# A ring of six weight places, with the low parts written over the weights

## The reference, cut to what matters

```
def reference(x, mem, ...):
    h = first_block(x, mem, ...)       # depth 1
    return second_block(h, ...)        # depth 2, then rmsnorm

first_block:   proj = rmsnorm(h) @ w_in                      # q, k, v, u
               h += concat(norm(attention(q, k, v)), norm(s5(u))) @ w_out
               h += memory_attention(rmsnorm(h), rmsnorm(mem))   # w_mem_q, _k, _v, _o
               h += peer(rmsnorm(h))
peer:          q = x @ w_peer_q;  scores against 2 x 128 keys, top 16 x 16 of 16384 experts
               sum_k gate[k] * gelu(x . u[k]) * v[k]
hybrid_layer:  proj = rmsnorm(x) @ w_in                      # 9 parts
               mixed = sum of 3:  sigmoid(gate) * (mixer(proj) @ w_mixer_out)   # ssd, mla, gdn
               h = x + mixed @ w_out
               return h + square(relu(rmsnorm(h) @ w_up)) @ w_down
```

## Time and profile before

| | |
|---|---|
| median of 3 runs | 5157.57 us (5157.56 to 5158.48) |
| profiled execution: its time, its span | 5149.14 us, 5147.2 us |
| mean granted TensorE clock, share of full speed | 0.983 |
| busy: PE, DVE, ACT, POOL | 4939.9, 2903.8, 1800.2, 704.3 us |
| DMA | 527.60 MB, mean 103 GB/s |

### The profile page before, as it was taken

The page is one execution under the profiler, slowest core; times in us unless marked ns, Lnnn a source line. Parts: engine busy times, 40 slices in busy tenths (PEclk is TensorE's granted clock), DMA queues, the critical chain, the costliest instruction groups (busy, mean ns, idle before and its releaser), DMA issues. The chain is left out here.

```text
span 5147.2 us, 62486 instructions
## 1 busy us (share of the span) xinstructions
PE 4939.9 (96%) x24184; PEld 4029.3 (78%) x24184; DVE 2903.8 (56%) x5300; ACT 1800.2 (35%) x2840; POOL 704.3 (14%) x494
## 2 busy tenths in 40 slices
PE   8979999999999999998999999999989999999999
PEld 6438688888887888877887777888878877777887
DVE  6676568888403544456546555553474466565533
ACT  3314433333322322233333334342333333343422
POOL 4641002233240000000300001000003100011000
PEclk9989999999999999998999999999999999999999
DMA  2012133555546555531022121322210221213222
GB/s 107 25 45 95 49 112 116 188 184 187 181 152 216 188 196 191 193 135 42 1 80 73 61 74 49 112 91 98 90 54 1 74 72 64 70 54 107 90 99 82
DMA packets 231733, 527.60 MB, mean 103 GB/s; under 512 B 19600, under 2 KB 89488, under 8 KB 230032
## 3 DMA queue, kind: packets, MB, share of 16 engines
q1 hardware_dynamic: 231440, 523.61, 29.9%
HBM read 448.03 MB, written 75.50 MB: 102 GB/s over the span
## 5 line engine op out<-in xcount | busy, mean ns | idle before, releaser
L552 DVE TENSOR_TENSOR weight_low<-ring,weight_high 128x1024 fp32r<-128x1024 f32 (+2 forms) x606 | 709.2, 1170 | 1230.0 <-PE banks L105 1164.8
L540 ACT CAST weight_high<-ring 128x1024 fp32r<-128x1024 f32 (+2 forms) x728 | 728.2, 1002 | 546.9 <-PE banks L105 518.9
L103 PE MATMUL banks<-x_high,weight_high 128*128 128x512 f32 x1856 | 758.7, 409 | 30.2 <-DVE weight_low L552 17.1
L552 POOL TENSOR_TENSOR weight_low<-ring,weight_high 128x1024 fp32r<-128x1024 f32 x122 | 301.0, 2468 | 3288.6 <-PE banks L105 2135.5
L105 PE MATMUL banks<-x_high,weight_low 128*128 128x512 f32 x1856 | 727.4, 392 | 0.0
L104 PE MATMUL banks<-x_low,weight_high 128*128 128x512 f32 x1856 | 727.0, 392 | 0.0
L103 PEld LDWEIGHTS banks<-x_high,weight_high 128*128 128x128 f32 x1856 | 351.3, 189 | 123.1 <-issue 26.8
L104 PEld LDWEIGHTS banks<-x_low,weight_high 128*128 128x128 f32 x1856 | 351.3, 189 | 82.0 <-issue 10.6
L103 PE MATMUL banks<-xn_high,weight_high 128*128 128x512 f32 x1024 | 410.5, 401 | 0.7 <-ACT hT L1744 0.7
L105 PEld LDWEIGHTS banks<-x_high,weight_low 128*128 128x128 f32 x1856 | 350.8, 189 | 74.6
L103 PE MATMUL banks<-act_high,weight_high 128*128 128x512 f32 x1024 | 399.0, 390 | 5.6 <-DVE act_low L1976 5.6
(11 more groups left out here) (638 smaller groups left out, 9099.1 us busy)
## 6 DMA issues: line engine op xcount, KB each, us to landing
ring<-in_peer_u SPq DMA_DIRECT2D x128, 512.0 KB, 3.3
ring<-in_peer_v SPq DMA_DIRECT2D x128, 512.0 KB, 3.4
acts<-dot_act SPq DMA_DIRECT2D x128, 256.0 KB, 2.0
gates<-gate_block SPq DMA_DIRECT2D x64, 512.0 KB, 4.6
ring<-in_w_up SPq DMA_DIRECT2D x64, 512.0 KB, 3.2
ring<-in_w_down SPq DMA_DIRECT2D x64, 512.0 KB, 3.2
activations<-acts SPq DMA_DIRECT2D x126, 256.0 KB, 3.7
gates_in<-gates SPq DMA_DIRECT2D x126, 256.0 KB, 3.9
```

Source lines behind the costliest of these rows:

```text
L103: nc.tensor.matmul(out, w_high, x_high, start=start, stop=False)
L540: self.nc.scalar.copy(self.wH[:, g % HIGHS, 0:kc * P], self.ring[:, g % SLOTS, 0:kc * P]).then_inc(self.high_made, 1)
L552: ops.tensor_tensor(self.wL[:, g % LOWS, 0:kc * P], self.ring[:, g % SLOTS, 0:kc * P], self.wH[:, g % HIGHS, 0:kc * P].bitcast(F32), ALU.s ...
```

## The change

The ring grows from four places to six, and the room for `weight_low` (two places) goes. The low part of tile g is written over the tile itself, in place g % 6. `ring_low` is a second name for the ring's memory, in the type that TensorE takes. So a load waits until TensorE has used tile g - 6, and a low part waits for nothing but its high part. In `linears` and `combine`, DVE makes both low parts of the stage that comes next, and POOL none. Whoever borrows the ring is given its first four places. There are now six semaphores for loads and six for low parts, where there were four and two.

```diff
-HIGHS, LOWS = 3, 2
+HIGHS, RING = 3, 6
@@ Weights
-        self.wL = held.enter_context(nc.sbuf_tensor("weight_low", [P, LOWS, D], F32R))
+        self.nc, self.ring, self.wL = nc, ring, ring_low
...
-        if g >= SLOTS:
-            self.wait_low(sp, g - SLOTS)
-        sp.dma_start(self.ring[:, g % SLOTS, 0:kc * P], row(w, at)).then_inc(self.loaded[g % SLOTS], 16)
+        if g >= RING:
+            sp.wait_ge(self.used, g - RING + 1)
+        sp.dma_start(self.ring[:, g % RING, 0:kc * P], row(w, at)).then_inc(self.loaded[g % RING], 16)
...
         eng.wait_ge(self.high_made, g + 1)
-        if g >= LOWS:
-            eng.wait_ge(self.used, g - LOWS + 1)
-        ops.tensor_tensor(self.wL[:, g % LOWS, 0:kc * P], self.ring[:, g % SLOTS, 0:kc * P],
-                          self.wH[:, g % HIGHS, 0:kc * P].bitcast(F32), ALU.subtract).then_inc(self.low_made[g % LOWS], 1)
+        ops.tensor_tensor(self.wL[:, g % RING, 0:kc * P], self.ring[:, g % RING, 0:kc * P],
+                          self.wH[:, g % HIGHS, 0:kc * P].bitcast(F32), ALU.subtract).then_inc(self.low_made[g % RING], 1)
@@ linears, gpsimd
-            if ahead:
-                weights.split_low(eng, nc.gpsimd, ahead.kc, base + total + 1)
@@ linears, vector
             for i in range(total):
-                if i + 2 <= total:
-                    lows(eng, nc.vector, i + 2)
-                elif ahead:
-                    weights.lows += 1
+                lows(eng, nc.vector, i + 2)
@@ combine
-            @block.gpsimd
-            def _(pool):
-                weights.split_low(pool, nc.gpsimd, ahead.kc, base + PK + 1)
...
                 weights.split_low(dve, v, ahead.kc)
-                weights.lows += 1
+                weights.split_low(dve, v, ahead.kc)
@@ program
-        ring = sb("ring", [P, SLOTS, 8 * P])
+        ring_at = nc.sbuf_base
+        ring = sb("ring", [P, RING, 8 * P])
+        ring_low = nc.alloc_sbuf_tensor_at("ring_low", [P, RING, 8 * P], F32R, offset=ring_at)
```

More of the change, by code:

```diff
@@ L508, with __init__ @@
 class Weights:
-    def __init__(self, nc, held, ring):
+    def __init__(self, nc, held, ring, ring_low):
         def sem(name):
             return held.enter_context(nc.semaphore(name))
-        self.nc, self.ring = nc, ring
+        self.nc, self.ring, self.wL = nc, ring, ring_low
         self.wH = held.enter_context(nc.sbuf_tensor("weight_high", [P, HIGHS, D], F32R))
-        self.wL = held.enter_context(nc.sbuf_tensor("weight_low", [P, LOWS, D], F32R))
-        self.loaded = [sem(f"weight{u}_loaded") for u in range(SLOTS)]
+        self.loaded = [sem(f"weight{u}_loaded") for u in range(RING)]
         self.high_made, self.used = sem("weight_high_made"), sem("weight_used")
-        self.low_made = [sem(f"weight_low{u}_made") for u in range(LOWS)]
+        self.low_made = [sem(f"weight_low{u}_made") for u in range(RING)]
         self.loads = self.highs = self.lows = self.placed = 0
@@ L530, in load @@
         g, self.loads = self.loads, self.loads + 1
-        if g >= SLOTS:
-            self.wait_low(sp, g - SLOTS)
-        sp.dma_start(self.ring[:, g % SLOTS, 0:kc * P], row(w, at)).then_inc(self.loaded[g % SLOTS], 16)
+        if g >= RING:
+            sp.wait_ge(self.used, g - RING + 1)
+        sp.dma_start(self.ring[:, g % RING, 0:kc * P], row(w, at)).then_inc(self.loaded[g % RING], 16)
     def split_high(self, act, kc):
         g, self.highs = self.highs, self.highs + 1
-        act.wait_ge(self.loaded[g % SLOTS], 16 * (g // SLOTS + 1))
+        act.wait_ge(self.loaded[g % RING], 16 * (g // RING + 1))
         if g >= HIGHS:
             act.wait_ge(self.used, g - HIGHS + 1)
-        self.nc.scalar.copy(self.wH[:, g % HIGHS, 0:kc * P], self.ring[:, g % SLOTS, 0:kc * P]).then_inc(self.high_made, 1)
+        self.nc.scalar.copy(self.wH[:, g % HIGHS, 0:kc * P], self.ring[:, g % RING, 0:kc * P]).then_inc(self.high_made, 1)
     def wait_low(self, eng, g):
-        eng.wait_ge(self.low_made[g % LOWS], g // LOWS + 1)
+        eng.wait_ge(self.low_made[g % RING], g // RING + 1)
     def split_low(self, eng, ops, kc, at=None):
@@ L549, in split_low @@
         eng.wait_ge(self.high_made, g + 1)
-        if g >= LOWS:
-            eng.wait_ge(self.used, g - LOWS + 1)
-        ops.tensor_tensor(self.wL[:, g % LOWS, 0:kc * P], self.ring[:, g % SLOTS, 0:kc * P],
-                          self.wH[:, g % HIGHS, 0:kc * P].bitcast(F32), ALU.subtract).then_inc(self.low_made[g % LOWS], 1)
+        ops.tensor_tensor(self.wL[:, g % RING, 0:kc * P], self.ring[:, g % RING, 0:kc * P],
+                          self.wH[:, g % HIGHS, 0:kc * P].bitcast(F32), ALU.subtract).then_inc(self.low_made[g % RING], 1)
     def parts(self, g, c):
         w = slice(c * P, (c + 1) * P)
-        return self.wH[:, g % HIGHS, w], self.wL[:, g % LOWS, w]
+        return self.wH[:, g % HIGHS, w], self.wL[:, g % RING, w]
     def clear(self):
@@ L948, in attention_memory @@
     return (scratch[:, 3:5, :], scratch[:, 5:8, :],
-            ring[:].rearrange("p s n -> p (s n)").rearrange("p (b k n) -> p b k n", b=2, k=4), spare[:, 0, 0:8])
+            ring[:, 0:SLOTS, :].rearrange("p s n -> p (s n)").rearrange("p (b k n) -> p b k n", b=2, k=4), spare[:, 0, 0:8])
 MIXED_FROM = 6
@@ L1457, in state_space @@
                                           tables.bim)
-    sets = [scratch[:], ring[:].rearrange("p s (two n) -> p (s two) n", two=2)]
+    sets = [scratch[:], ring[:, 0:SLOTS, :].rearrange("p s (two n) -> p (s two) n", two=2)]
     def by_half(x):
@@ L2646, in delta_rule @@
         kb = yT[:].rearrange("p c (t n) -> p c t n", n=P)[:, 4:8]
-        ring4 = ring[:].rearrange("p s (a t n) -> p s a t n", t=TT, n=P)
+        ring4 = ring[:, 0:SLOTS, :].rearrange("p s (a t n) -> p s a t n", t=TT, n=P)
         Dm = [ring4[:, 0, 0], ring4[:, 0, 1]]
@@ L2939, in program @@
         rstd = sb("rstd", [P, T])[:]
-        weights = Weights(nc, held, ring)
+        weights = Weights(nc, held, ring, ring_low)
         tools = (roots, eps, ident[:], columns, ones[:])
```

## The result

The kernel after takes 5191.28 us (median of 4 runs, 5190.06 to 5192.77) against 5157.57: ratio 1.0068, 95% interval 1.0056 to 1.0080. It is 0.7% slower; 5143.8 was forecast. The profiled execution took 5190.61 us, 41.5 more than that of before.

The account below looks back on a forecast made before the run. TensorE, busy 4939.9 of 5147.2 us, was taken as the bound. Stage ends 8.2 plus stalls inside stages 6.0 less clears 0.4 gave 13.8 us less: median 5143.8 from 5157.57, range 5138 to 5149, chance 0.70.

Parts of the forecast that it names:

- Writing in place.: DVE's low parts written over their source: from -0.02 to +0.02 us per low part, taken as 0.
- The rival on the slow side: DVE becomes last at the 16 stage-end barriers, late by a low part of 1.23 us: 5171.7 us, chance 0.04.
- all eight like rows 3: Eight stage ends like mem_in's, where POOL's low part comes last: idle 0.85 becomes 0.30, 4.4 us saved.
- mla_tail, two ends: Two stage ends where DVE comes last, slowed beside POOL: it ends 0.94 us sooner each, 1.9 saved.
- latents, two ends: Ends of the latents' stage: the new DVE low part delays the last eviction, yet restart comes sooner; 1.4 us saved.
- mem_in, first stall: Eviction in mem_in no longer stands behind a waiting low part; the 1.60 us stall shrinks by 1.1.
- gdn_tail, two layers: Low parts start without DVE's idle time of 0.47; the 2.82 us stall shrinks by 0.7, twice: 1.4 saved.
- ssd_tail, two layers: Stall of 2.10 us becomes 1.34, and the half-clock stretch behind it probably goes; 1.3 each, 2.6 saved.
- combine, 0.88: Low part in combine starts up to 3.01 us earlier, so TensorE's 0.88 wait for activations goes: 0.9 saved, once.
- six more clears: Six added semaphores are cleared at the program's end: cost 0 to 0.55 us, taken as 0.4.
- Stage ends: POOL's 16 low parts at stage ends go and DVE takes them over, shortening TensorE's idle time: 8.2 us saved together.
- gdn_in: Low part there starts with no idle time before it, so its stalls stay; nothing was counted.

Follow-up runs that it names:

- low_aligned: The kernel after with the table `columns` moved ahead of the ring, so low parts start at a multiple of 256 bytes: 5133.79 us, ratio 0.9959 to before.
- before_low_swapped: The kernel before with low parts placed ahead of the high parts, both at a multiple of 256 bytes: 5154.63 us, ratio 0.9997.
- aligned_pool_ends: The kernel after with aligned low parts, POOL again making the second low part at 16 stage ends, without waiting for TensorE: 5132.68 us, ratio 0.9958.
- pool_ends_late: The kernel after with aligned low parts, POOL making those 16 stage-end low parts and again waiting for TensorE's use two tiles before: 5143.62 us, ratio 0.9983.

## Why the prediction was wrong

**The step that failed: "Writing in place."** The prediction asked what the low part costs DVE, and got that right: "I take 0", and the mean of one 128x1024 low part on DVE is 1234 ns after and 1233 before. It never asked what the new place costs those who read from it. Each of the 5408 chunks of low parts that meet 512 columns is loaded by TensorE, the engine that bounds the kernel, and the sum took its matmuls as unchanged. That left out +62.7 us, more than four times the whole forecast gain. Nor could the prediction's sign for this term, a low part of more than 1.23 alone, have caught it: it, too, looks only at the engine that makes the low part. A row of before could not have priced it, since every operand of a product started at a multiple of 256 there. But the changed start could be worked out from the allocations, and the range should then have had an unknown for it on the slow side.

**The rival on the slow side** had the right sign and the wrong mechanism. It had DVE last at the 16 barriers, late by a whole low part. None of the 13 restarts that were priced waits longer than before, and all eight like rows 3 have 0.30.

**The rest of the sum, read in low_aligned,** where the steps are as before:

| term | forecast | low_aligned, profiled |
|---|---|---|
| eight ends like mem_in | 4.4 | 8 x 0.55 = 4.4 |
| mla_tail, two ends | 1.9 | 2 x 0.94 = 1.9 |
| latents, two ends | 1.4 | 0.94 + 0.80 = 1.7 |
| combine's end | 0.5 | 0.8 |
| mem_in, first stall | 1.1 | 1.60 - 0.36 = 1.2 |
| gdn_tail, two layers | 1.4 | 2 x (0.39 + 0.54) = 1.9, and 2.9 behind it, less 2 x 1.7 of clock = 1.4 |
| ssd_tail, two layers | 2.6 | 2 x 0.2, and 2 x 1.7 of clock = 3.8 |
| combine, 0.88 | 0.9 | 0.9 |
| mix_in's end, 1.59 | 0 | 1.59 - 0.33 = 1.3 |
| mix_out, a wait for POOL's mixed_low | 0 | 0.25 - 0.69 = -0.4 |
| six more clears | -0.4 | -0.1 |
| together | 13.8 | 16.9 |

Its profiled execution is 15.9 us below that of before, that of its repetition 20.1; the medians are 21.6 and 25.0 below. Executions of one kernel differ by several us (15 of before on one chip took 5148.84 to 5161.10), so the table can't be read to tenths. One place where they differ: in the first attention the profile of before, on which the prediction was built, lacks a stall of 4.65 to 4.69 us that the other 13 profiles have. This is the row in before_low_swapped, whose instructions are those of before:

```profile
161.69 1.97 PE L1009 MATMUL banks<-ring,vS 128*64 128x512 f32 x2 [4.68 <-ACT ring L1076]
```

- *Stage ends*: right in size. The cause was put too broadly: POOL's 2.35 us made it last only together with the wait for TensorE. Without the wait POOL costs nothing there (aligned_pool_ends against pool_ends_late); with the wait, a POOL low part of 1.27 cost nothing either.
- *gdn_tail*: the 2.82 became 2.28 where 2.1 was forecast. Two things were missed: a small stall of 0.39 one tile earlier went, and so did one of 1.47 and 1.43 further on, which waited for DVE's gdn_y_low. Part of this was lost to the clock, as the next point shows.
- *ssd_tail*: the stall fell from 2.10 to 0.90, lower than the 1.34 forecast, but the tile behind it then waited 1.00. The low part beside POOL's norm stayed long, as the prediction had it:

```profile
3244.58 6.04 POOL L327 TENSOR_TENSOR ssd_y_low<-hT,ssd_y_high 128x512 fp32r<-128x512 f32 x4 [4.20 <-ACT ssd_y_high L294]
3247.12 2.35 DVE L549 TENSOR_TENSOR ring_low<-ring,weight_high 128x1024 fp32r<-128x1024 f32 x1 [3.80 <-ACT weight_high L539]
```

By the rule of the Trainium skill that was cited there ("SBUF — State Buffer", section "Who interferes with whom"), the trace agrees: 2.35 beside POOL, 1.22 alone. What was won here is the clock. Busy us by stretch behind the two stalls of low_aligned, the column behind POOL's being the granted clock:

```profile
3242.00:3245.40 3.40, 2.62 (x11) 2.18 (x12) 1.33 (x2) 2.04 (x4) 0.82 (x1) 1.00 0.46 154
3249.00:3252.40 3.40, 2.88 (x13) 2.38 (x14) 1.76 (x3) 1.57 (x2) 1.62 (x1) 1.00 0.47 154
```

It is 1.00 in both, where it was 0.50 behind the one stall of before. But the same was lost in gdn_tail. These are the stretches of low_aligned behind the stalls of 2.28 and 2.27, one in each layer:

```profile
2732.10:2735.50 3.40, 3.40 (x9) 2.65 (x9) 1.70 (x4) 2.19 (x3) 0.00 (x0) 0.50 0.03 10
4155.50:4158.90 3.40, 3.40 (x8) 2.73 (x9) 1.85 (x3) 2.14 (x3) 0.00 (x0) 0.51 0.07 27
```

Before, the clock behind the stalls of 2.82 and 2.83 there was 1.00. The repetition and the four other runs with all operands aligned and early low parts show the same exchange, so the clock gave nothing in sum. The prediction reasoned that an idle time shorter than 2.82 would leave the clock at 1.00. It came out at ssd_tail, but that was luck: in gdn_tail 2.28 did not.

- *gdn_in* kept its stalls, as forecast: 0.32, 1.00 and 1.61.

So the stage ends and the stalls moved as forecast, POOL's part was put too broadly, and the clock term came out by luck; all of them together are about a third of what the address cost.

## What to carry to other kernels

When a change moves what the bounding engine reads, work out the new start addresses and treat a change of their remainder as an unknown cost on every instruction that reads there; here TensorE's products lost time at both starts tried off a multiple of 256 bytes (128 and 192 past one). When the busy time of an engine grows at the same count and clock, look at the steps of a stretch without stalls before looking at waits. And when a low-priority engine ends last at a barrier, ask first what it waits for, and only then whether it is too slow.

## What the runs showed of the hardware

- A float32 product (fp32r) of 512 columns steps at 227 ns when weights and moving operand start at a multiple of 256 bytes in their partitions. With weights that start 128 bytes past one, the steps in which they load or run are 232 to 235 ns; with a moving operand so placed, 232 in the median. Low parts 64 bytes lower than the aligned ones cost the same in sum (61 us against 62.7), in steps of 224 to 241; a multiple of 512 gives no more than one of 256.
- In products of 256 columns shifted low parts showed no loss: their steps behind L104 average 124.0 before and 122.7 after.
- The length of an idle time alone did not tell the clock behind it: behind 2.82 us in gdn_tail the granted clock stayed at 1.00 (before), behind 2.28 at the same place it was 0.50 for 3.40 us (low_aligned).
- A tensor_tensor on DVE whose output lies over one of its inputs takes as long as one that writes elsewhere: 1234 against 1233 ns.
